# Low parts of five operands start at other places modulo 256 bytes than their high parts

## What is computed

```python
h = h + (o * silu(r)) @ gla_w_out              # GLA's output      (272 tokens)
h = h + (silu(gate) * up) @ ffn_w_out[0]       # gated MLP 0       (272 tokens)
h = h + attention1 @ dsa_w_out                 # attention 1
h = h + (silu(gate) * up) @ ffn_w_out[1]       # gated MLP 1
h = h + (gelu(gate) * lru) @ a_w_out           # recurrent block
h = h + square(relu(x @ w_up[l])) @ w_down[l]  # MLP 0 and 1 of the second block
```

## The kernel before

| tensor | rows apart | start before | start after |
|---|---|---|---|
| `w_hi`, `w_lo` (every tile) | 512 | 128 | 128 |
| `x_hi`, `x_lo`, rows of all 272 tokens | 1280 | 64 | 64 |
| the same, 256 tokens of a 272-token row (attention 1's inputs) | 1280 | 128 | 128 |
| row 7 of either | | 128, 192 | 128, 192 |
| `x_hi`, `x_lo`, row 7 in the layout `xs` of 256-token rows | | 128 | 128 |
| the same, other rows of `xs` and all of `xl` | 1024 | 64 | 64 |
| `ga_hi` / `ga_lo` (GLA's output) | 1280 | 64 / 64 | 64 / 192 |
| `mid_hi` / `mid_lo` (both gated MLPs) | 1280 | 64 / 64 | 64 / 128 |
| `at_hi` / `at_lo` (attention 1's output) | 1024 | 64 / 64 | 64 / 0 |
| `lr_hi` / `lr_lo` (recurrent block's output) | 1024 | 64 / 64 | 64 / 128 |
| `m_hi` / `m_lo` (middles of MLP 0 and 1) | 1024 | 64 / 64 | 64 / 192 |
| `c_hi` / `c_lo` (attention 1's latent), rows 0 and 1 | 1088 | 64, 128 / 192, 0 | the same |

## Time and profile before

### The profile page before, as it was taken

How to read it: one execution, slowest core, us unless ns; L and a number is a source line. 1 busy time by engine, 2 the same in 40 slices (tenths; PEclk the granted TensorE clock), 3 DMA queues, 4 the chain that set the end, 5 groups by cost and what they waited for, 6 DMA issues and landing times.

```text
span 1185.0 us, 25998 instructions
## 1 busy us (share of the span) xinstructions
PE 1172.1 (99%) x9738; PEld 1144.0 (97%) x9738; DVE 820.7 (69%) x1301; ACT 693.4 (59%) x1120; POOL 89.4 (8%) x97
## 2 busy tenths in 40 slices
PE   8999999999999999999999999999999999999998
PEld 8999999999998999999999989999999979999998
DVE  7767866665668877666669997665467677766543
ACT  6635665644445666665557976554447576666432
POOL 1000200000100020000120000000013233000000
PEclk9999999999999999999999999999999999999999
DMA  7533655556664336666665555656666424666663
GB/s 274 173 107 92 192 178 177 177 176 195 190 209 125 107 127 191 193 193 190 216 210 169 167 174 196 184 192 181 198 196 220 129 88 146 192 193 189 206 194 106
DMA packets 57578, 207.85 MB, mean 175 GB/s; under 512 B 6352, under 2 KB 7568, under 8 KB 57248
## 3 DMA queue, kind: packets, MB, share of 16 engines
q1 hardware_dynamic: 57136, 203.52, 54.6%
q0 software_dynamic: 288, 3.21, 0.7%
q10 hardware_dynamic: 80, 0.07, 0.0%
HBM read 205.66 MB, written 1.05 MB: 174 GB/s over the span
## 4 chain that ended last, share of the span: by engine, by line
PE 90%; ACT 4%; DVE 3%; issue 1%; DMA 1%; SPq 0%; ACTq 0%; DVEq 0%
PE acc L1008 27%; PE acc L1010 26%; PE acc L1009 26%; DVE w_lo L1697 1%; ACT w_hi L512 1%; PE acc L1143 1%; PE acc L1551 1%; PE acc L1598 1%; PE acc L1359 1%; DMA w_raw<-weights 1%; DVE x_lo L1717 0%; PE acc L1553 0%; PE acc L1552 0%; PE pt L1584 0%; PE pa L1265 0%
## 5 line engine op out<-in xcount | busy, mean ns | idle before, releaser
L1697 DVE TENSOR_TENSOR w_lo<-w_raw,w_hi 128x1024 fp32r<-128x1024 f32 x379 | 463.1, 1224 | 69.9 <-ACT w_hi L512 69.4
L512 ACT CAST w_hi<-w_raw 128x1024 fp32r<-128x1024 f32 x379 | 395.0, 1045 | 175.2 <-PE acc L1010 173.6
L1008 PE MATMUL acc<-x_hi,w_hi 128*128 128x256 f32 (+1 forms) x1688 | 479.0, 284 | 1.7 <-DVE w_lo L1697 1.1
L1009 PE MATMUL acc<-x_lo,w_hi 128*128 128x256 f32 (+1 forms) x1688 | 474.5, 281 | 0.0
L1010 PE MATMUL acc<-x_hi,w_lo 128*128 128x256 f32 (+1 forms) x1688 | 474.1, 281 | 0.0
L1008 PEld LDWEIGHTS acc<-x_hi,w_hi 128*128 128x128 f32 x1688 | 317.5, 188 | 5.0 <-DVE x_lo L1717 1.7
L1010 PEld LDWEIGHTS acc<-x_hi,w_lo 128*128 128x128 f32 x1688 | 318.7, 189 | 0.0
L1009 PEld LDWEIGHTS acc<-x_lo,w_hi 128*128 128x128 f32 x1688 | 317.7, 188 | 0.5
L1008 PE MATMUL acc<-m_hi,w_hi 128*128 128x256 f32 x512 | 142.6, 278 | 0.0
L1009 PE MATMUL acc<-m_lo,w_hi 128*128 128x256 f32 x512 | 142.6, 278 | 0.0
L1010 PE MATMUL acc<-m_hi,w_lo 128*128 128x256 f32 x512 | 142.6, 278 | 0.0
(11 more groups left out here) (372 smaller groups left out, 1683.4 us busy)
## 6 DMA issues: line engine op xcount, KB each, us to landing
w_raw<-weights SPq DMA_DIRECT2D x381, 512.0 KB, 3.9
bias<-bias_rows POOLq DMA_DIRECT2D x1, 2048.0 KB, 11.2
h<-hT SPq DMA_DIRECT2D x4, 272.0 KB, 4.5
bias<-bias_rows POOLq DMA_DIRECT2D x1, 1088.0 KB, 8.7
outT<-h SPq DMA_DIRECT2D x4, 256.0 KB, 4.8
con<-constants SPq DMA_DIRECT2D x1, 913.0 KB, 9.0
w_raw<-weights SPq DMA_DIRECT2D x2, 256.0 KB, 3.5
par<-cols SPq DMA_DIRECT2D x1, 84.0 KB, 2.0
```

What stands on the lines that cost most here:

```text
L512: nc.scalar.copy(w_hi[:, slot, :], w_raw[:, slot, :]).then_inc(hi_ready, 1)
L1008: nc.tensor.matmul(out, wh, xh[:, k, tok], start=first and n == 0, stop=False)
L1009: nc.tensor.matmul(out, wh, xl[:, k, tok], start=False, stop=False)
L1697: V.tensor_tensor(w_lo[:, slot, :], w_raw[:, slot, :], w_hi[:, slot, :].bitcast(F32), ALU.subtract)\
```

## The change

Five unused tensors are allocated, each between the high and the low part of an operand. They are of 128, 64, 192, 64 and 128 bytes of a partition. The low part begins that much later, and so does everything that is allocated behind it in the same region (in GLA's region `k_T` to `o_rs`, in the gated MLPs' `sqg`). No instruction is added, removed or moved on any engine; nothing but addresses differs. `x_hi` and `x_lo` and attention 2's `xq_hi` and `xq_lo` stay where they are.

```diff
         ga_hi = get("ga_hi", [P, KD, ROW], F32R)
+        ga_gap = get("ga_gap", [P, 32])
         ga_lo = get("ga_lo", [P, KD, ROW], F32R)
@@
         mid_hi = get("mid_hi", [P, 24, ROW], F32R)
+        mid_gap = get("mid_gap", [P, 16])
         mid_lo = get("mid_lo", [P, 24, ROW], F32R)
@@
         at_hi = get("at_hi", [P, ATT_HEADS, SEQ], F32R)
+        at_gap = get("at_gap", [P, 48])
         at_lo = get("at_lo", [P, ATT_HEADS, SEQ], F32R)
@@
         lr_hi = get("lr_hi", [P, KD, SEQ], F32R)
+        lr_gap = get("lr_gap", [P, 16])
         lr_lo = get("lr_lo", [P, KD, SEQ], F32R)
@@
         m_hi = get("m_hi", [P, FF2T, SEQ], F32R)
+        m_gap = get("m_gap", [P, 32])
         m_lo = get("m_lo", [P, FF2T, SEQ], F32R)
```

## The result

The changed kernel took 1192.68 us, median of 9 runs (1191.27 to 1196.09); the kernel before took 1186.87 us in 9 runs beside it (1181.88 to 1189.87). The ratio is 1.0073, with a 95% interval of 1.0051 to 1.0094: slower by 0.7%. The forecast was 1190.7 us, in a range of 1181.5 to 1198.5.

The account below looks back on a forecast made before the run. TensorE, busy 99% of the span, was taken to bound the kernel through its time per matmul. Costs for `mid`, `m`, `at`, `lr` and the 272-column stretches summed to +3.8 us on 1186.9, giving 1190.7 us, range 1181.5 to 1198.5.

Parts of the forecast that it names:

- Nothing but the pace can change: TensorE is busy 99% of the span, so a change of addresses alone can act only through the time per matmul.
- No gain is to be had where the pace is fast: No 256-column stretch runs under 113.0 ns a matmul, so stretches at the fast pace have nothing shown to gain.
- 5.7 ns for each low matmul: Assumed cost of each moved low-part matmul at 256 columns, from 119.0 against 113.3 ns; 20 ns at most.
- the excursion: Matmuls starting elsewhere among others at 64: three at shifted row 7 cost 20 ns; after the change, every third matmul.
- rival C: Full excursions: every triple costs near 20 ns, as at row 7; +9 to +13.5 us, 1198 us; chance 0.14.
- `m` of MLP 0 stays where it is: Already at the slow pace, 117.8 ns, so taken as 0; +1.7 us if it rises, -3.4 us if it turns fast.
- 272 columns, +1 ns from the latent's products: First gated MLP's `mid` and `ga`: +1.0 ns a matmul, as the latent's mixed starts showed; +0.7 us.
- A stretch of `x` may change its pace by chance: Unchanged `x` stretches keep one of two paces; a switch, 4.4 ns a matmul, belongs to chance, not the change.
- Rival A: Mixed starts knock TensorE out of the slow pace, `m` of MLP 0 gains 3.4 us; 1183 us; chance 0.28.
- Its reading of the earlier trace: Attention 2's value products run fast, six steps in 0.68 us, so a low part at 192 may equal 64.
- Rival B: No difference: each stretch keeps its pace, set once at its start; 1186.9 us; chance 0.20.
- The sign of being wrong that names `x`: The prediction is wrong if the pace of `x` stretches follows from how the stretch ahead ended.

Follow-up runs that it names:

- shift_mlp: Kernel before, with the second group of four input units in MLP 0 and MLP 1 written out, reading row 7 shifted: 1181.10 us, ratio 0.9975.
- shift_mlp_lru: As shift_mlp, and all units of the recurrent block's input read row 7 at its shifted place: 1183.05 us, ratio 0.9992 against the kernel before.

## Why the prediction was right

The forecast was +3.8 us and the medians differ by 5.8; the sign and the places hold, the size in part by luck, as the last step tells. Step by step:

- **Nothing but the pace can change.** Right: the table above accounts for 5.8 of 5.9 us by paces alone.
- **No gain is to be had where the pace is fast.** Right; no kernel here showed a 256-column stretch under 113.0 ns.
- **5.7 ns for each low matmul.** Too little, and this is the term that was mis-sized. `mid` paid 5.8 ns on every matmul, 17 ns a triple, `m` of MLP 1 4.5 and 13.5, `at` 5.0 (5.4 by the single starts) and 15 or 16. One product in three lies elsewhere, and yet all three pay (by the single starts the three steps of `mid` take 121.1, 118.9 and 117.8 ns): the excursion costs nearly what it did at row 7 (20 ns), a part of it behind the low matmul, and I had taken the shorter excursion to be the cheaper. `mid` +3.1 us against 1.0, `m` of MLP 1 +3.5 against 1.5, `at` +1.0 against 0.4, `lr` +0.6 against 0.2. Against rival C, which had 13.5 us for all, the truth lies nearer to it than to the forecast in `mid` (3.1 of 3.5 us), and midway in `m` of MLP 1 (3.5, between 1.5 and 5.1).
- **`m` of MLP 0 stays where it is.** Right in the number, 117.8 before and after, and not by my reason, that it stood at the slow pace already. The `x` ahead of it was fast in the changed kernel, and `m` went to 117.8 from there, just as in MLP 1: it is the pace of this pair of starts. In executions of before where it was fast, it should lose 3.4 us as MLP 1 does.
- **272 columns, +1 ns from the latent's products.** Right: 0.8 to 0.9 ns, +0.6 us against 0.7.
- **A stretch of `x` may change its pace by chance.** It did, -3.0 us in the profiled pair. Without it the five changed tensors cost 8.8 us. That is why the medians came within 2 us of the forecast: terms too small by 5 us together, and a stretch that happened to be fast in one profile and slow in the other. The groups of runs say the same without a profile. Those of the changed kernel lie 3.1 us apart, which is `x` of MLP 0 alone (3.0), since its `m` paces 117.8 either way; and group against group the change costs 8.2 to 9.2 us, more than twice the forecast. The profiles would have 8.8 for the longer groups and 12.2 for the shorter ones (3.4 more for `m` of MLP 0); of the latter 3 us are not found in the runs, of which the kernel before has only three there. The two groups of before, and their absence in shift_mlp, show that the state is the execution's and not the change's.

Rival A fell by half. A shifted row does end the slow pace (shift_mlp_lru), but a mixture in every triple is no such cure: it has no fast pace of its own, with any of the three pairs tried. Its reading of the earlier trace rows was also too wide: attention 2's value products pace 113.3 ns in those six steps, but 117.8 in most of their units (939.04 to 939.75 us, six steps in 0.71). Rival B fell with `mid`. The sign of being wrong that names `x` didn't come: in the trace of before `x` of MLP 0 is fast up to 712 us and slow behind a wait of its own, so its pace doesn't follow from how the stretch ahead ended.

The Trainium skill (SBUF — State Buffer, "Who interferes with whom") has TensorE's two read ports independent and never waiting. The runs disagree: with the weights moved by 64 bytes, and no row that TensorE reads, it took 1220.91 us, against 1182.62 us of the kernel before on the same chip. Whatever the two reads meet in, they are not independent here.

What stays open is the mechanism: which resource the row's read and the weights' read share, why 64 bytes of distance have two states, what in a wait chooses between them, and why `m` behind a slow `x` is the faster one with the low part at 128 (117.7 against 119.4) and the slower one with the rows at 0 (120.1 against 118.6). Nor did I try a weight part that begins elsewhere than its other part, or a second start between 64 and 96.

## What to carry to other kernels

Where one engine streams without a gap, read the distance between starts, stretch by stretch, before anything else: a few ns a matmul are invisible in busy shares (99% in both kernels) and made 38 us in one kernel here. Lay out all the rows that are streamed in alternation at one and the same distance from the weights' start modulo 256 bytes, and measure that distance for each number of columns; do not vary one of them. Compare medians only after a look at the single runs, since two groups in each kernel made 5.8 us here of a cost of 8 to 9. If equal code on equal addresses paces differently between executions, look for a state, and put the one disturbance that ends it (here a row shifted by 64 bytes) behind the last wait, more than once.

## What the runs showed of the hardware

- One shape of matmul (256 float32r columns) paced from 113.3 to 120.1 ns by nothing but where row and weights begin modulo 256 bytes; equal starts are the dearest. With 272 columns it paced from 123.1 to 126.8, and there equal starts (125.1) are cheaper than a distance of 128 (126.6). A move by a full 256 bytes changes nothing (113.1 and 123.1 ns with the gap of 256).
- At 64 bytes ahead of the weights or beyond them the same instructions hold 113.3 or 117.8 ns, for tens of us on end; 113.3 beyond them was seen for 2 to 3 us at a time only. Nine of 23 executions of the kernel before were some 6 us longer than the rest, which is what MLP 0 at 117.8 costs.
- A stretch takes over the state of the one before it where no wait lies between: where `x` paced 117.8 in MLP 0 and 113.3 in MLP 1, their `m` differed too (four of four profiles); where the two `x` paced alike, so did the two `m` (ten of ten).
- A row shifted by 64 bytes ends the slow pace, in seven profiles at the first such row and in two at the second; in the recurrent block it took 116.4 ns a matmul to 114.4.
